# Three layers with experts: an earlier bias row, pool-engine sums, a hybrid layer reordered, and the last expert pair written out behind the loop

## What is computed

```python
# layers 0 and 1 (first_block)
sh1, sc1, g1, sh2, sc2, g2 = split(silu(c) @ ada_w[i] + ada_b[i], 6)
h = rms_norm(x, norm_mix_g[i]) * (1 + sc1) + sh1
y = diff_attention(h, ..., t5_bias) if i == 0 else chunked_attention(h, ..., rel_bias)
x = x + g1 * y
h = rms_norm(x, norm_ffn_g[i]) * (1 + sc2) + sh2
x = x + g2 * grouped_moe(h, ...)     # 16 experts, d_ff 512, two picked for a token
# third layer (hybrid_layer), with 256 context tokens xc
h  = rms(x) * norm1_w * (1 + sc1) + sh1
hc = rms(xc) * norm1_w * (1 + mod_c[1]) + mod_c[0]
p, pc = h @ w_in, hc @ w_in[:, OFF_KV:OFF_G]
ya = chunk_mlp(p[..., :OFF_B], w_s, b_s)        # u * (w_s @ rms(v)), with gelu on u and v
yb = latent_attention(q, k, v, kc, vc)          # 8 heads, 2 kv heads, keys of tokens and context
yc = hgrn_out(hgrn_bidir(...), ...)             # two gated scans
x  = x + g1 * (concat(ya, yb, yc) @ w_out)
x  = x + g2 * hier_moe(h2, ...)      # 32 experts, d_ff 512, two picked for a token
# an expert: (silu(t @ w_gate) * (t @ w_up)) @ w_down, weighted by its gate
```

## Time and profile before

| | |
|---|---|
| time, median of 3 runs | 1627.34 us (1625.66 to 1629.7) |
| the profiled execution: its time | 1624.21 us |
| its span | 1622.4 us |
| mean granted TensorE clock | 0.977 |
| PE busy | 1572.2 us (97%) |
| DVE busy | 546.8 us (34%) |
| ACT busy | 395.3 us (24%) |
| POOL busy | 52.0 us (3%) |
| moved by DMA | 535.25 MB, mean 330 GB/s |

### The profile page before, as it was taken

The page is one execution under the profiler, slowest core; times in us unless marked ns, Lnnn a source line. Parts: engine busy times, 40 slices in busy tenths (PEclk is TensorE's granted clock), DMA queues, the critical chain, the costliest instruction groups (busy, mean ns, idle before and its releaser), DMA issues.

```text
span 1622.4 us, 21352 instructions
## 1 busy us (share of the span) xinstructions
PE 1572.2 (97%) x8569; PEld 899.0 (55%) x8569; DVE 546.8 (34%) x1319; ACT 395.3 (24%) x861; POOL 52.0 (3%) x65
## 2 busy tenths in 40 slices
PE   7989999999999999999999999888999999999998
PEld 3655675444456747644545876567645445454454
DVE  3453532322244262432222265442332312323122
ACT  2142321111131432411211353352311112111121
POOL 0000000000000001000000034001000000000000
PEclk9999989999999999999999999799899999999999
DMA  9898759999997778599999400521599999999995
GB/s 356 326 343 308 304 237 425 429 429 429 428 374 280 291 287 321 238 427 426 430 428 416 166 1 2 210 102 46 231 426 429 429 428 429 428 429 428 429 429 225
DMA packets 94820, 535.25 MB, mean 330 GB/s; under 512 B 7951, under 2 KB 11881, under 8 KB 70194
## 3 DMA queue, kind: packets, MB, share of 16 engines
q1 hardware_dynamic: 94354, 534.39, 80.9%
q10 hardware_dynamic: 416, 0.17, 0.0%
HBM read 533.48 MB, written 1.06 MB: 329 GB/s over the span
## 4 chain that ended last, share of the span: by engine, by line
PE 89%; DMA 6%; ACT 2%; DVE 2%; issue 1%; SPq 1%; POOL 0%; DVEq 0%; POOLq 0%; ACTq 0%
PE pair L1026 26%; PE bank L1013 7%; PE pair L1033 6%; PE bank L755 6%; PE bank L1033 6%; DMA ring<-in_w_dram 4%; PE bank L1075 3%; PE pair L1075 3%; PE bank L652 3%; PE pair L1103 3%; PE bank L849 2%; PE bank L762 2%; PE pair L731 2%; PE bank L1103 1%; DMA ring<-in_a_w_qkv_dram 1%; PE pair L665 1%
## 5 line engine op out<-in xcount | busy, mean ns | idle before, releaser
L1026 PE MATMUL pair<-ring,arena 128*64 128x512 f32 x2048 | 447.2, 594 | 0.6 <-DMA ring<-in_w_dram 0.6
L1026 PEld LDWEIGHTS pair<-ring,arena 128*64 128x64 f32 x2048 | 144.3, 137 | 285.3 <-issue 284.9
L2352 DVE TENSOR_TENSOR arena<-sq,pair 128x512 f32<-128x512 f32 x32 | 33.9, 1060 | 387.0 <-PE pair L1026 387.0
L1013 PE MATMUL bank<-arena 128*128 128x128 f32 x1120 | 141.3, 282 | 3.2 <-DVE arena L2234 3.2
L1013 PEld LDWEIGHTS bank<-arena 128*128 128x128 f32 x1120 | 135.6, 198 | 3.5 <-issue 3.4
L755 PE MATMUL bank<-hh,ring 128*128 128x256 f32 x512 | 115.9, 382 | 1.1 <-DMA ring<-in_a_w_qkv_dram 1.1
L1033 PE MATMUL pair<-ring,arena 128*64 128x512 f32 x512 | 116.9, 598 | 0.0
L1033 PE MATMUL bank<-ring,arena 128*64 128x512 f32 x512 | 115.3, 592 | 0.0
L1708 ACT ACTIVATE sq<-pair 128x512 f32<-128x512 f32 x32 | 19.1, 597 | 367.5 <-PE pair L1026 367.5
L755 PEld LDWEIGHTS bank<-hh,ring 128*128 128x128 f32 x512 | 95.6, 190 | 23.5 <-issue 7.6
L2360 DVE COPY arena<-bank 128x512 f32<-128x512 f32 x32 | 22.1, 691 | 181.1 <-PE bank L1033 181.1
(11 more groups left out here) (408 smaller groups left out, 1702.6 us busy)
## 6 DMA issues: line engine op xcount, KB each, us to landing
ring<-in_w_dram SPq DMA_DIRECT2D x96, 2048.0 KB, 15.0
ring<-in_moe_w_gate_dram SPq DMA_DIRECT2D x32, 2048.0 KB, 11.8
ring<-in_moe_w_up_dram SPq DMA_DIRECT2D x32, 2048.0 KB, 15.8
ring<-in_moe_w_down_dram SPq DMA_DIRECT2D x32, 2048.0 KB, 14.3
ring<-in_ada_w_dram SPq DMA_DIRECT2D x24, 2048.0 KB, 16.9
ring<-in_w_mod_dram SPq DMA_DIRECT2D x12, 2048.0 KB, 12.4
ring<-in_a_w_qkv_dram SPq DMA_DIRECT2D x6, 2048.0 KB, 20.2
ring<-in_b_w_qkv_dram SPq DMA_DIRECT2D x6, 2048.0 KB, 16.8
```

Source lines behind the costliest of these rows:

```text
L1013: last = mm(b[part][:, cols(k % 4)], h_tok[:, t, cols(k)], pick_n[:, t, :], start=(t == 0), stop=(t == TT - 1))
L1026: last = mm(b[2 + m][half(a), :], x_sel[:, k, half(a)], R8[moe_slot(l, a, m)][:, k, :], start=(k == 0), stop=(k == KT - 1))
L2352: tt(hid.rearrange("p (f q) -> p q f", f=FT), by_row(gate_act), by_row(b[3]), ALU.mult).then_inc(M["hid_ready"], 1)
```

## The change

1. **T5 row.** PE's matmul for it moves up, behind the first batch of modulations; ACT's copy moves behind the first of the four `queries`. SP issues load 10 before it waits for the row, and load 11 behind the bias read.
2. **Sums of squares.** At the start of layer 1 and for the context norm POOL adds the pieces, and PE does one matmul instead of eight: in layer 1 behind the products for k=5, for the context behind the first gathers. POOL's counts shift (15 becomes 29, 22 becomes 36).
3. **Hybrid layer.** ACT copies `sc_rows` before the Gelu of `vm`, takes the Sqrt behind the copies of `sc`, and does `turned_copy(2)` before the Gelu of `u`. PE runs `scores(0)` ahead of the transposes of `sc_rows`, `scores(7)` ahead of `values(2)`, and `transposes(7)` between the two halves of `out_first(3)`.
4. **Last pair.** `nit` is one lower; the loops run over all pairs but the last, and the body is written out once more behind each loop, without the gathers, picks and evacuations for a next pair. The waits for `sel_a` and `sel_b` of such a pair are gone.

```diff
@@ -489,15 +489,13 @@
...
-            for n in range(6, 10):
+            for n in range(6, 11):
                 load(n)
             sp.wait_ge(t5_row, turn(t5_row))
             sp.dma_start(t5_dram, t5row).then_inc(t5_out, 16)
-            for n in range(10, 12):
-                load(n)
             sp.wait_ge(t5_out, 16)
             sp.dma_start(bias[:, 0:8, :], bass.AP(t5_dram.tensor, 0, [[1, P], [512, 8], [1, S]])).then_inc(bias_in, 16)
-            for n in range(12, 18):
+            for n in range(11, 18):
                 load(n)
             for dst, src in const_loads:
@@ -698,10 +696,10 @@
...
-            def summed_squares(l):
+            def summed_squares(steps):
 
                 turn(sq_ready, KT)
-                pe.wait_ge(pool_step, (7, 14, 22)[l])
+                pe.wait_ge(pool_step, steps)
                 mm(b[4][:, 0:S], ones, sq[:, 0:S], start=True, stop=True).then_inc(ssq_ps, 1)
@@ -871,12 +869,12 @@
...
                 mods(A[0])
+                if l == 0:
+                    mm(b[5][0:8, :], t5b, bucket, start=True, stop=True).then_inc(t5_ps, 1)
                 project(3, 0)
                 mods(A[1])
                 project(4, 0)
                 project(5, 0)
@@ -999,9 +997,6 @@
...
-                if l == 1:
-                    for k in range(KT):
-                        square_sum(k)
@@ -1039,9 +1034,11 @@
...
+                if l == 1:
+                    summed_squares(28)
                 pe.wait_ge(n_ready, l + 1)
-                n = pe.value_load(nit[0:1, 0:1], min_val=1, max_val=ROUNDS * EXPERTS[l] // 2)
-                with pe.Fori(0, n) as i:
+                m = pe.value_load(nit[0:1, 0:1], min_val=1, max_val=ROUNDS * EXPERTS[l] // 2 - 1)
+                def pair_of(i, last_pair):
                     pe.wait_ge(M["sel_a"], i + 1)
                     project(i, 0)
                     project(i, 1)
@@ -1050,14 +1047,16 @@
...
-                    pe.wait_ge(M["pick_ready"], 2 * i + 4)
-                    gather(0)
+                    if not last_pair:
+                        pe.wait_ge(M["pick_ready"], 2 * i + 4)
+                        gather(0)
                     pe.wait_ge(M["hid_ready"], i + 1)
                     pe.wait_ge(M["added"], 4 * i + 2)
...
                         last = nc.tensor.transpose(b[4][:, cols(f)], hid[:, cols(f)], ident)
...
-                    gather(1)
+                    if not last_pair:
+                        gather(1)
@@ -1075,14 +1074,16 @@
...
-                pe.wait_ge(M["sel_a"], n + 1)
-                pe.wait_ge(M["sel_b"], n + 1)
+
+                with pe.Fori(0, m) as i:
+                    pair_of(i, False)
+                pair_of(m, True)
...
-                pe.wait_ge(M["added"], n * 4 + 2)
+                pe.wait_ge(M["added"], m * 4 + 6)
@@ -1293,19 +1294,22 @@
...
-                def out_first(n):
-                    if n == 0:
+                def out_first(n, only=None):
+                    if only == 1:
+                        pass
+                    elif n == 0:
...
-                    for c in (2 * n, 2 * n + 1):
+                    for c in (2 * n, 2 * n + 1) if only is None else (2 * n + only,):
                         for k in range(4):
                             last = mm(b[6][:, c % 2 * S:(c % 2 + 1) * S], w[:, k, cols(c)], ymix[:, k, :],
                                       start=(k == 0), stop=(k == 3))
-                    last.then_inc(out_proj, 2)
+                    if only != 0:
+                        last.then_inc(out_proj, 2)
@@ -1404,13 +1408,13 @@
...
                 double_keys(1)
+                scores(0)
 
...
                 last.then_inc(sc_ps, 1)
-                scores(0)
                 turn_scores(0)
@@ -1438,18 +1442,19 @@
...
                 transposes(5)
+                scores(7)
                 values(2)
-                scores(7)
                 out_first(2)
                 transposes(6)
-                out_first(3)
+                out_first(3, 0)
                 transposes(7)
+                out_first(3, 1)
                 values(3)
...
-                summed_squares(2)
+                summed_squares(36)
@@ -1487,8 +1492,8 @@
...
                             first_values(1, t, k)
-                        for j in range(*((0, 0), (0, 3), (3, 6), (6, 8))[k] if k < 4 else (0, 0)):
-                            square_sum(j)
+                        if k == 5:
+                            summed_squares(14)
@@ -1622,9 +1627,9 @@
...
-                if l == 0:
-                    act.wait_ge(t5_ps, 1)
-                    fn(t5row, b[5][0:8, :], ACT.Copy).then_inc(t5_row, 1)
+                    if l == 0 and i == 0:
+                        act.wait_ge(t5_ps, 1)
+                        fn(t5row, b[5][0:8, :], ACT.Copy).then_inc(t5_row, 1)
@@ -1699,22 +1704,27 @@
...
-                n = act.value_load(nit[0:1, 0:1], min_val=1, max_val=ROUNDS * EXPERTS[l] // 2)
+                m = act.value_load(nit[0:1, 0:1], min_val=1, max_val=ROUNDS * EXPERTS[l] // 2 - 1)
...
-                with act.Fori(0, n) as i:
+                def pair_of(i, last_pair):
...
-                    act.wait_ge(M["gather_a"], i + 2)
-                    first()
+                    if not last_pair:
+                        act.wait_ge(M["gather_a"], i + 2)
+                        first()
...
-                act.wait_ge(M["added"], n * 4 + 2)
+
+                with act.Fori(0, m) as i:
+                    pair_of(i, False)
+                pair_of(m, True)
+                act.wait_ge(M["added"], m * 4 + 6)
@@ -1828,17 +1838,17 @@
...
+                act.wait_ge(sc_ps, 2 * SUB)
+                fn(sc_rows, b[7][:, 0:S], ACT.Copy).then_inc(act_step, 1)
                 act.wait_ge(in_ready, EVAC["vm1"])
                 fn(vm, vm, ACT.Gelu_apprx_tanh).then_inc(in_ready, 1)
-                act.wait_ge(sc_ps, 2 * SUB)
-                fn(sc_rows, b[7][:, 0:S], ACT.Copy).then_inc(act_step, 1)
-                act.wait_ge(vm_sums, 1)
-                fn(vm_stat[:, 8:16], vm_stat[:, 0:8], ACT.Sqrt, bias=eps[:, :], scale=1.0 / HEAD).then_inc(vm_rt, 1)
...
                 last.then_inc(sc_ready, 1)
+                act.wait_ge(vm_sums, 1)
+                fn(vm_stat[:, 8:16], vm_stat[:, 0:8], ACT.Sqrt, bias=eps[:, :], scale=1.0 / HEAD).then_inc(vm_rt, 1)
@@ -1859,9 +1869,9 @@
...
                 act.wait_ge(ssq_ps, turn(ssq_ps))
                 root(b[6][0:32, 0:S], rt[0:32, :], HEAD, 32)
+                turned_copy(2)
                 act.wait_ge(in_ready, EVAC["u1"])
                 fn(uT, uT, ACT.Gelu_apprx_tanh).then_inc(in_ready, 1)
-                turned_copy(2)
@@ -1916,8 +1926,7 @@
...
-            def sum_squares(l):
-                first, done = (KT, 3 * KT, 6 * KT)[l], (0, 7, 15)[l]
+            def sum_squares(first, done):
...
-            sum_squares(0)
-            sum_squares(1)
+            sum_squares(KT, 0)
+            sum_squares(2 * KT, 7)
+            sum_squares(3 * KT, 14)
+            sum_squares(4 * KT, 21)
@@ -2313,7 +2324,7 @@
...
-                ts(nit[:, 0:1], r["most"], E / 2.0, E / 2.0, ALU.mult, ALU.add).then_inc(n_ready, 1)
+                ts(nit[:, 0:1], r["most"], E / 2.0, E / 2.0 - 1.0, ALU.mult, ALU.add).then_inc(n_ready, 1)
@@ -2339,23 +2350,25 @@
...
-                with dve.Fori(0, n) as i:
-                    nxt = bass.ds(2 * i + 2, 2)
-                    dve.wait_ge(M["gather_b"], i + 1)
-                    dve.wait_ge(M["pickg_ready"], i + 1)
-                    pick_pair(nxt)
-                    dve.wait_ge(M["pick_ready"], 2 * i + 3)
-                    expert_pick_normed(l)
+                def pair_of(i, last_pair):
+                    if not last_pair:
+                        nxt = bass.ds(2 * i + 2, 2)
+                        dve.wait_ge(M["gather_b"], i + 1)
+                        dve.wait_ge(M["pickg_ready"], i + 1)
+                        pick_pair(nxt)
+                        dve.wait_ge(M["pick_ready"], 2 * i + 3)
+                        expert_pick_normed(l)
...
                        ALU.mult).then_inc(M["hid_ready"], 1)
                     dve.wait_ge(M["gate_turned"], i + 1)
-                    dve.wait_ge(M["pick_ready"], 2 * i + 4)
-                    gate_pair(nxt)
-                    dve.wait_ge(M["gather_b"], i + 2)
-                    second().then_inc(M["sel_b"], 1)
+                    if not last_pair:
+                        dve.wait_ge(M["pick_ready"], 2 * i + 4)
+                        gate_pair(nxt)
+                        dve.wait_ge(M["gather_b"], i + 2)
+                        second().then_inc(M["sel_b"], 1)
...
+
+                with dve.Fori(0, m) as i:
+                    pair_of(i, False)
+                pair_of(m, True)
```

14 lines of the change are left out of this document (6 added, 8 removed).

## The result

The changed kernel takes **1611.3 us** (median of 5 runs, 1607.8 to 1616.9) against 1629.63 us before (5 runs); the ratio is 0.9903, 95% interval [0.9884, 0.9922], which is -15.8 us [-18.9, -12.7] (the two medians alone lie 18.3 apart; the ratio with its interval is what is used here). The forecast was 1613.2 us, or -14.1. The profiled execution took 1612.74 us, with a span of 1611.0 us and a mean granted clock of 0.978. Against the profiled execution before that is only -11.4 of span.

What follows compares the result with a forecast made beforehand. PE's stream plus its few waits bounds the kernel; weight transfers pace the third layer's experts. Terms -3.3 - 4.8 - 3.0 - 0.3 - 0.5 - 2.2 = -14.1 give 1610.1, 1613.2 us for the median; range 1606 to 1619.

Steps and rivals of the forecast that it cites:

- Rival 3: Third layer's experts: transfers set the pace, loads do not start earlier, earlier savings return as waits; about -3, 1624; chance 0.06.
- T5 row, -3.3: Loads at the start: load 10 no longer waits for the row, chunk 13 lands at 93.5 instead of 96.8; -3.3 us.
- PE waits 1.5: T5 row term: PE is ready for chunk 13 at 92.0, it lands at 93.5, so PE waits 1.5 us.
- upper end, -4.9: T5 row bound: if the write could overtake load 10 and nothing holds the bias up, -4.9 us.
- Last pairs, -4.8: Last pair of each layer: without gathers, the chain from hid to down is 1.6 us shorter, three times; -4.8 us.
- they are there at 1602.7, just ahead of 1602.85: Third layer's last pair: the two down chunks land at 1602.7, before down begins at 1602.85.
- Squares at the start of layer 1, -3.0: Start of layer 1: POOL adds the squares, one PE matmul stays of eight, nobody waits for the root; -3.0 us.
- Context squares, -0.3: Layer 1's context: eight matmuls of 5.17 us go, but gathers slow from 3.69 to 6.4 at lower clock; -0.3 us.
- Hybrid, -0.5, 0, -2.2: Hybrid layer: transposes moved behind scores(0), -0.5; turned_copy(2) sooner, 0; waits before the last two values filled, -2.2 us.
- Rival 1: More gain: bias not held up, clock stays up at the context's gathers and hybrid start; about 1607.7; chance 0.13.
- Rival 2: Savings mostly become waits: half clock behind them at the last pairs, layer 1's start loses to h; -8.5, 1618.8; chance 0.10.
- Rival 4: Loops of layers 1 and 2: moved code makes all 22 turns fetch instructions; +18, 1645, slower; chance 0.05.

Runs made afterwards that it cites:

- the two kernels with filler: Changed kernel with gather(1) kept on PE alone in the third layer's last pair: 0.9903; the second also with the T5 row written by ACT's queue: 0.9874.
- the one with gathers: Changed kernel with a next pair's gathers, picks and evacuations put back in the third layer's last pair alone: 0.9911.

## Why the prediction was right, and where it was not

A single trace holds chance in the clock, so here the thirteen traces are split into those with a part and those without, and their means compared (us; in brackets the number of traces; the third line, end of up to second half of down, is taken from the table of last pairs, without the two kernels with filler and the one with gathers):

| stretch | forecast | without | with | mean difference |
|---|---|---|---|---|
| start to layer 0's first gathers (T5 row) | -3.3 | 227.6 (4) | 225.0 (7) | -2.6 |
| first project to second half of last down, layers 0 and 1 | -3.2 for both | 224.26 (4) | 222.57 in 13 of 18, 224.27 in 5 | -1.2 each, -2.4 |
| the same pair, third layer | -1.6 | 7.8 | 7.3 (6) | -0.5 |
| second half of layer 0's last down to layer 1's qkv products (squares) | -3.0 | 28.77 (4) | 25.75 (9) | -3.0 |
| end of ranks to first project, layer 1 (context) | -0.3 | 9.0 (5) | 7.8 (8) | -1.2 |
| second half of layer 1's last down to first head | -0.5 | 152.6 (4) | 151.3 (9) | -1.2 |
| first head to `values(1)` | 0 | 37.5 (4) | 37.3 (9) | -0.2 |
| `values(1)` to `values(3)` | -2.2 | 29.6 (4) | 27.3 (9) | -2.3 |
| `values(3)` to the third layer's first project | 0 | 39.6 (4) | 38.9 (9) | -0.7 |

- **What bounds it** (PE's stream plus its waits; the third layer's experts moved as a whole): right. First project to down in the last pair of that layer took 453.5 us before and 452.9 now, so the lead from before passed through it. Rival 3, a stage that doesn't move, is out.
- **T5 row, -3.3**: the mechanism was right: the write lay behind load 10 (13.8 us), and the gap is 3.0 us. The step that was short is "PE waits 1.5": PE waited 1.8 to 2.7, and most often paid 1.7 more for it at half clock. Measured alone -2.3 [-3.7, -1.0]; by places -2.6. The prediction's upper end, -4.9 if nothing holds the bias up, is what the write on ACT's queue reached (5.8 by places, of which 2.6 are the change's own); it was counted there as a rival, without asking which edit would bring it about.
- **Last pairs, -4.8**: where the clock held, layers 0 and 1 gave 1.7 each, by the very chain (hid, turned, copy), with waits of 0.9 and 0.7. What the term put at nothing is the clock behind these waits: in five of the 18 pairs it took the 1.7 back. In the third layer "they are there at 1602.7, just ahead of 1602.85" left no room: a late chunk and half clock made it a loss of 1.1 in one execution and 0.4 in another; in the four others without gathers or filler it was a gain of 0.8 to 1.7; the mean over the six is a gain of 0.5. So the three pairs are -2.9 on average; this part alone measured -3.7 [-5.0, -2.3], with no pair at half clock in its trace.
- **Squares at the start of layer 1, -3.0**: 3.0 in every trace. Each POOL addition took 0.91 from start to start and not 0.72 to 0.8; with 4 us in hand that changed nothing.
- **Context squares, -0.3**: right in mechanism: the gathers at a granted clock near 0.6 gave most of the removed work back. The size was short: from the start of the gathers to the first project 6.9 us were set; it took 5.5 in four traces and 6.4 to 7.1 in four. (The working of this term, 667.3 against 667.5, gives 0.2.) That is 1.2 by places; the measurement with this part undone can't tell it from nothing.
- **Hybrid, -0.5, 0, -2.2**: 1.2, 0.2 and 2.3 by places, and 0.7 more behind them, where the prediction has no term. In eight of the nine traces with this part the tokens are turned at full clock in the route (2.0 us), in none of the four without it (3.3 to 3.7); the gathers behind give 0.4 back. So this gain goes with the part, though no work in the route changed; by what means was not tested. Alone the part measured -4.2 [-5.7, -2.8].
- **Rival 1** (more than that): 1607.7 is what the kernel with the write on ACT's queue takes (1606.77), which the change is not. Its other half, a better clock at the context's gathers and at the hybrid start, came in part, 0.9 and 0.7 us beyond the forecast. **Rival 2** was right in its mechanism: waits in the place of gathers did bring half clock, in seven of 24 pairs (five of 18 in layers 0 and 1, two of six in the third), though its "against" was that the waits here are under 2, and 0.91 and 0.69 us they are. It was wrong in how often, and in the start of layer 1, which lost nothing. **Rival 4** (jumps): two more fetches in all, none a turn; not slower.
- **The sum**: -14.1 against -15.8 [-18.9, -12.7], inside the interval. The stretches of the table add up to -14.1 too, and that is luck: 0.7 too much at the row and 1.9 at the last pairs, 0.9 too little at the context, 1.0 in the hybrid layer and 0.7 in the route behind it. Most of these misses come with the clock that PE was granted, and not with the order of the work.

## What to carry to other kernels

Here a small transfer on which a large one depended stood behind megabytes of prefetch on the same queue: the order of the issues was not the order of need, and a second queue was worth more (some 5 us) than moving the issue (2.3). Work removed beside a chain is worth what the chain gets shorter, not its own length; write down what ends last there afterwards, and how many tenths of a us it has in hand, above all against transfers that only just arrive. And count a wait of PE with what may follow it: in these traces the products behind a wait over 2 us ran at half clock in six of seven cases, and `down` behind two waits of 0.9 and 0.7 us in five of 18.

## What the runs showed of the hardware

- **Fetches of PE's instructions delay weights.** One 16 KB packet occupied its transfer engine for about 1.07 us by its record. Of nine traces with such a fetch in or just ahead of the third layer's last pair, a chunk landed 5.6 to 6.2 us behind the one before, instead of 4.9, in six; in one it was 0.4 us late, in two not at all. In the kernel before, a fetch at 1499.2 us, earlier in the same stage, also has a chunk land 5.5 us behind the one before. That adding PE work moved both is shown; why two chunks came in time is open. With 36 fetches in a run, nearly all outside the loops, this matters only where a chunk is just in time. The Trainium skill, page "Runtime: NRT & Kernel Launch", section "Instruction fetch mechanics", tells of such blocks of 16 KiB; the fetched packets of 16 KB here agree.
- **A small write on a second queue** took 5.2 us from issue to landing beside busy transfers, behind a load on the same queue 13.8, on idle engines 1.5.
- **The granted clock isn't a function of the code.** The same 16 products, behind the same wait of 2.73 us, took 3.69 us in one kernel and 5.38 in two others that don't differ there. The first half of `down`, behind the same waits of 0.91 and 0.69 us, took 3.65 us in 13 pairs and 5.35 in five. And before 60 us, where the code is the same, the first qkv products began at 48.93 us in the kernel before's trace and at 52.23 in the changed kernel's, where the squares ahead of them ran in part at half clock (3.19 us for eight matmuls instead of 1.99) and the loads came later. Single traces can't price a change under 3 us here; places between two fixed operations can, and best as a mean over several traces.
